# A hybrid decoder block on one core: two experts' weights loaded in shifted halves, the router's and the final norm's small loads moved, and the first tile's slots ahead of the second's

## The reference, cut to what matters

```python
h = concat(meta_tokens, x)                  # 16 + 256 positions of 1024
u = rmsnorm(h, norm_mix_w)
p = u @ w_in                                # 1024 x 7184: pool, q, k, v, z, a, b, two gates
merged = sigmoid(g_A) * pool_mixer(p) + sigmoid(g_B) * gated_deltanet(p)
h = h + merged @ w_out
u = rmsnorm(h, norm_ffn_w)
group  = argmax(softmax(u @ router_group_w + router_group_b))           # 4 groups
expert = top2(softmax((u @ router_expert_w + router_expert_b)[group]))  # 8 in the group
h = h + sum_e weight_e * ((silu(u @ w_gate[e]) * (u @ w_up[e])) @ w_down[e])   # 32 experts
out = rmsnorm(h, norm_final_w)[16:]         # all float32
```

## Time and profile before

| | us |
|---|---|
| median of three runs | 775.12 |
| the profiled execution's own time | 776.95 |
| span of the profile | 775.2 |
| TensorE busy | 748.8 (97%) |
| VectorE busy | 320.9 (41%) |
| ScalarE busy | 311.9 (40%) |
| GpSimd busy | 125.4 (16%) |
| DMA queue of SP, share of 16 engines | 81.2% |

### The profile page before, as it was taken

How to read it: one execution, slowest core, us unless ns; L and a number is a source line. 1 busy time by engine, 2 the same in 40 slices (tenths; PEclk the granted TensorE clock), 3 DMA queues, 4 the chain that set the end, 5 groups by cost and what they waited for, 6 DMA issues and landing times.

```text
span 775.2 us, 16094 instructions
## 1 busy us (share of the span) xinstructions
PE 748.8 (97%) x6512; PEld 536.1 (69%) x6512; DVE 320.9 (41%) x793; ACT 311.9 (40%) x632; POOL 125.4 (16%) x209
## 2 busy tenths in 40 slices
PE   8999999999999999899999999999999999998895
PEld 7989989998999988655555555565555555454452
DVE  4894687678675855822211311220221112111112
ACT  6975678586584744712212121222112121121123
POOL 7473242225433540000000000000000000000000
PEclk9999999999999999999999999999999999999999
DMA  8536556554754458999999999999999999999993
GB/s 204 147 87 165 152 135 160 138 151 110 181 147 125 140 193 309 414 400 424 420 427 428 428 427 428 425 429 426 428 427 427 428 427 426 429 426 426 424 416 137
DMA packets 83552, 241.06 MB, mean 311 GB/s; under 512 B 7185, under 2 KB 65666, under 8 KB 71826
## 3 DMA queue, kind: packets, MB, share of 16 engines
q1 hardware_dynamic: 83170, 239.19, 81.2%
q10 hardware_dynamic: 304, 0.79, 0.4%
HBM read 238.92 MB, written 1.05 MB: 310 GB/s over the span
## 4 chain that ended last, share of the span: by engine, by line
PE 80%; DMA 11%; issue 4%; DVE 4%; ACT 1%; POOL 0%; SPq 0%; DVEq 0%; POOLq 0%; ACTq 0%
PE banks L2158 23%; PE banks L1811 21%; PE banks L2216 12%; DMA ring<-in_expert_w_up_dram 10%; PE banks L2089 3%; PE banks L2171 3%; PE banks L2007 2%; PE banks L1931 1%; PE banks L2192 1%; PE banks L1944 1%; PE banks L1992 1%; PE banks L1935 1%; DMA x<-in_x_dram 1%; PE banks L1969 1%; PE banks L1948 1%
## 5 line engine op out<-in xcount | busy, mean ns | idle before, releaser
L2158 PE MATMUL banks<-ring,bench 128*64 128x256 f32 x2048 | 240.0, 388 | 8.4 <-DMA ring<-in_expert_w_up_dram 6.2
L2158 PEld LDWEIGHTS banks<-ring,bench 128*64 128x64 f32 x2048 | 146.6, 134 | 108.8 <-issue 21.0
L1811 PE MATMUL banks<-rounded 128*128 128x256 f32 (+2 forms) x1320 | 194.1, 294 | 0.0
L1811 PEld LDWEIGHTS banks<-rounded 128*128 128x128 f32 x1320 | 168.5, 189 | 3.1
L1714 DVE TENSOR_TENSOR bench<-banks,bench 128x256 f32<-128x256 f32 x32 | 13.6, 425 | 259.5 <-PE banks L2158 172.2
L2216 PE MATMUL banks<-ring,bench 128*64 128x512 f32 x512 | 116.9, 598 | 0.6 <-ACT bench L1096 0.5
L1107 ACT ACTIVATE ysb<-banks 64x512 f32<-64x512 f32 x63 | 37.2, 591 | 147.2 <-PE banks L2216 146.5
L2216 PEld LDWEIGHTS banks<-ring,bench 128*64 128x64 f32 x512 | 34.1, 136 | 63.2 <-issue 59.4
L875 ACT ACTIVATE rounded<-room 128x1024 fp32r<-128x1024 f32 x64 | 67.4, 1054 | 23.2 <-PE banks L1811 15.1
L1096 ACT ACTIVATE bench<-banks 128x256 f32<-128x256 f32 x32 | 12.3, 384 | 146.9 <-PE banks L2192 146.9
L1333 DVE TENSOR_TENSOR rounded<-room,rounded 128x1024 fp32r<-128x1024 f32 x49 | 61.6, 1259 | 16.5 <-ACT rounded L875 15.5
(11 more groups left out here) (312 smaller groups left out, 867.0 us busy)
## 6 DMA issues: line engine op xcount, KB each, us to landing
ring<-in_expert_w_down_dram SPq DMA_DIRECT2D x28, 2048.0 KB, 26.7
ring<-in_expert_w_gate_dram SPq DMA_DIRECT2D x27, 2048.0 KB, 25.6
ring<-in_expert_w_up_dram SPq DMA_DIRECT2D x27, 2048.0 KB, 26.8
room<-in_w_in_dram SPq DMA_DIRECT2D x56, 512.0 KB, 4.3
ring<-in_expert_w_up_dram SPq DMA_DIRECT2D x16, 512.0 KB, 7.1
ring<-in_expert_w_down_dram SPq DMA_DIRECT2D x16, 512.0 KB, 7.1
ring<-in_expert_w_gate_dram SPq DMA_DIRECT2D x12, 512.0 KB, 5.8
room<-in_w_out_dram SPq DMA_DIRECT2D x8, 512.0 KB, 4.5
```

The costliest lines, as they stand in the source:

```text
L1811: ins = T.matmul(o, a, b[:, k, lo_at:L], start=(k == 0 and n == 0), stop=(k == KT - 1 and n == 2))
L2158: ins = T.matmul(pb[5 + c][half * 64:half * 64 + SLOTS, 0:256], xgT[:, q % ROOMS, kt, j * SLOTS:(j + 1) * SLOTS], w[:, kt, half], start=(k ...
```

## The change: what it does

1. The final norm's gain is loaded as 8 columns (`gain_out`) at the start, and not spread by a DMA into `spare`. In experts 28 and 29 TensorE spreads it (`spread_gain`, 8 products each), and DVE copies it into `wfin`, which now lies in a part of `xgT` that is free by then.
2. The router's biases are loaded behind lands 10 and 11. The waits for biases and gains are one wait for four loads.
3. `FRONT_AFTER` lets the quarters of up 1 go one land earlier.
4. Chunks 9 to 14 (experts 3 and 4) are loaded in halves that are shifted by one half: 9a into `spare` after the logits, 9b into the first half of slot 0, 10a into its second half, and so on to 14b in the first half of slot 5. A semaphore `half` counts the first halves that TensorE has used.
5. In the router, DVE makes the first tile's slots before it picks for the second, the lows of tile 0 come before the slots of tile 1, and TensorE multiplies the first tile's high part before the second tile's place.

```diff
-ROUT = 5 * 16
+ROUT = 4 * 16
+SHIFTED = range(RING, RING + 6)          # RING = 9
+HALF_COUNTED = range(RING + 6)
-FRONT_AFTER = [61, 61, 62, 62]
+FRONT_AFTER = [60, 60, 61, 61]
+BIAS_AFTER = [10, 11]
...
+        def half_at(n, half, again):
+            if n in SHIFTED and not again:
+                at = 2 * (n - RING) + half - 1
+                if at < 0:
+                    return spare[:]
+            else:
+                at = 2 * (n % RING) + half
+            return ring[:, RING_AT[at // 2], at % 2 * CHUNK // 2:(at % 2 + 1) * CHUNK // 2]
...
+                if step == ("land", BIAS_AFTER[0]):
+                    sp.dma_start(rbias[:, 0:EXPERTS], router_expert_b[0:1, :].to_broadcast([P, EXPERTS])).then_inc(S("rout_land"), 16)
...
-                    sp.dma_start(rbias[:, 0:EXPERTS], router_expert_b[0:1, :].to_broadcast([P, EXPERTS])).then_inc(S("rout_land"), 16)
-                    sp.dma_start(rbias[:, EXPERTS:36], router_group_b[0:1, :].to_broadcast([P, GROUPS])).then_inc(S("rout_land"), 16)
-                    taken(sp, ("G", HEADS - 1))
-                    sp.dma_start(wfin, norm_final_w[None, :].to_broadcast([P, D])).then_inc(S("rout_land"), 16)
...
+                def used_up(n):
+                    sp.wait_ge(S(used[n % 3]), base + n // 3 + 1)
+                for n in range(3 * EXPERTS):
+                    e, c = n // 3, n % 3
+                    if n in SHIFTED and not again:
+                        if n == RING:
+                            sp.wait_ge(S("logits"), TT)
+                        else:
+                            used_up(n - RING - 1)
+                        if n >= RING + 3:
+                            sp.wait_ge(S(f"w_land{n - RING}"), 16 * loads_until(n - RING, False))
+                        load_half(sp, n, 0)
+                        sp.wait_ge(S("half"), n - RING + 1)
+                        load_half(sp, n, 1)
+                        continue
+                    if n >= RING:
+                        used_up(n - RING)
+                        if n - RING + 1 in SHIFTED and not again:
+                            sp.wait_ge(S("half"), n - RING + 2)
+                    elif again:
+                        sp.wait_ge(S(used[c]), base)
+                    if again or (e and (e, c) not in EARLY):
+                        load_chunk(sp, e, c)
...
             pick(0)
             inverse_rms(1)
+            first_slots(0)
             pick(1)
-            first_slots(0)
+            lows(0, front)
             first_slots(1)
-            for cols in (slice(0, 3 * D // PARTS), slice(3 * D // PARTS, D)):
-                for i in range(TT):
-                    lows(i, cols)
+            lows(1, front)
+            lows(0, rest)
+            lows(1, rest)
...
+                    elif j < GAIN_PARTS:          # DVE, experts 28 and 29
+                        dve.wait_ge(S("gathered"), parts + QUADS * PARTS + j + 1)
+                        V.tensor_copy(wfin[:, j * 512:(j + 1) * 512], pb[4][:]).then_inc(S("xgT"), 1)
...
             place(0)
             seed(0)
+            high_products(0)
             seed(1)
             place(1)
...
+                def spread_gain(n):
+                    pe.wait_ge(S("xgT"), parts + QUADS * PARTS + n - 2)
+                    for k in range(KT):
+                        ins = T.matmul(pb[4].rearrange("p (j k) -> p k j", k=KT)[:, k, :], gain_out[:, k:k + 1].to_broadcast([P, P]),
+                                       ident[:, n * 64:(n + 1) * 64], start=True, stop=True, skip_group_check=True)
+                    ins.then_inc(S("gathered"), 1)
...
                 def gather_first():
...
+                    pe.wait_ge(S("xlo"), 1)
+                    for part in range(PARTS - 1):
+                        first_products(xlo, part, 0)
+                    high_products(1)
+                    pe.wait_ge(S("xlo"), 2)
+                    for part in range(PARTS - 1):
+                        first_products(xlo, part, 1).then_inc(S("gathered"), 1)
...
                     for kt in range(KT):
...
-                        if first and (kt + 1) % (KT // QUARTERS) == 0 and kt < KT - 1:
-                            ins.then_inc(S("quarter"), 1)
+                        if kt == KT // 2 - 1 and 3 * e + c in HALF_COUNTED and not again:
+                            ins.then_inc(S("half"), 1)
...
                     turn_mid(e)
                     if q + 1 < QUADS:
                         gather(q + 1, j, 1)
+                    elif j < GAIN_PARTS:
+                        spread_gain(j)
```

More of the change, by code:

```diff
@@ L417, with loads_of, loads_until, loads_in_all @@
         LO_AT[_s[1]] = (_name, _i + 1)
-def uses(n, k, slots):
-    return (n - k + slots - 1) // slots
+def loads_of(n, again):
+    if (n // 3, n % 3) in PIECES or n < 3 and not again:
+        return 0
+    if n in SHIFTED and not again:
+        return 2
+    return QUARTERS if n in (3, 4) and not again else 1
+def loads_until(n, again):
+    return sum(loads_of(m, again) for m in range(n % RING, n + 1, RING))
+def loads_in_all(slot, again):
+    return sum(loads_of(m, again) for m in range(slot, 3 * EXPERTS, RING))
 def build_block(nc, x, meta_tokens, norm_mix_w, w_in, conv_w, pool_w, pool_scale, a_log, dt_bias, dn_norm_w,
@@ L812, in one_pass @@
                 again = not isinstance(ps, int)
[L813 to L821, removed]
-                                cols = slice(n * CHUNK // QUARTERS, (n + 1) * CHUNK // QUARTERS)
-                                slot = 3 * (e % RINGS) + c
-                                sp.dma_start(ring[:, RING_AT[slot], cols], (gate_v, up_v, down_v)[c][e][:, cols]).then_inc(S(f"w_land{slot}"), 16)
-                            continue
-                        if e >= RINGS:
-                            sp.wait_ge(S(used), base + (e - RINGS + 1))
-                        elif again:
-                            sp.wait_ge(S(used), base)
-                        if again or (e and (e, c) not in EARLY):
-                            load_chunk(sp, e, c)
@@ new lines, in one_pass @@
+                used = ("gate", "up", "y")
+                def used_up(n):
+                    sp.wait_ge(S(used[n % 3]), base + n // 3 + 1)
+                for n in range(3 * EXPERTS):
+                    e, c = n // 3, n % 3
+                    if n in SHIFTED and not again:
+                        if n == RING:
[16 more added lines that the diff above has]
+                        load_chunk(sp, e, c)
@@ L2130, in landed @@
-                    loads = ps * (uses(EXPERTS, e % RINGS, RINGS) - short) - (e % RINGS == 0)
-                    quarters = QUARTERS - 1 if e % RINGS == 0 or e % RINGS == 1 and (c < 2 or again or e > RINGS) else 0
-                    pe.wait_ge(S(f"w_land{3 * (e % RINGS) + c}"), 16 * (loads + quarters + (e // RINGS + 1)))
+                    n = 3 * e + c
+                    loads = loads_until(n, again)
+                    if again:
+                        first, other = (loads_in_all(n % RING, over) for over in (False, True))
+                        loads = ps * other + (first - other + loads)
@@ L2134, in gate_up @@
+                    pe.wait_ge(S(f"w_land{n % RING}"), 16 * loads)
                 def gate_up(e, c, name):
@@ L2210, in down @@
                         landed(e, 2)
[L2211 removed]
+                    ws = [half_at(3 * e + 2, n, again).rearrange("p (j d) -> p j d", j=2) for n in range(2)]
                     for j in range(4):
```

78 lines of the change are left out of this document (39 added, 39 removed).

## The result

| ten runs of each, same chip | median us | lowest to highest |
|---|---|---|
| kernel before | 775.27 | 774.88 to 776.66 |
| changed kernel | 777.63 | 776.65 to 779.07 |

The ratio is 1.003, with a 95% interval from 1.0022 to 1.0039: the change costs 2.3 us, between 1.7 and 3.0. The profiled execution of the changed kernel took 779.07 us (span 777.3), its slowest; the one of before took 776.95 (span 775.2). Both lie 1.4 to 1.8 above their medians, so the two traces can be set side by side; between them the span grew by 2.1 us. Chunk n is the load 3e + c of expert e, as in the code (c is 0 for gate, 1 for up, 2 for down); up 28 is the up matrix of expert 28, chunk 85. A landing is the start of an issue plus the view's time to landing, which has one decimal, so landings are good to 0.1 us.

A forecast was written before the change was run, and what follows sets the result against it. Expert-weight transfers were taken to bound the kernel, with TensorE's work after the last chunks behind them. Stream +0.2 and gain spreads +1.6 made +1.8 us on 775.12, giving 776.9 us, range 774.5 to 778.4.

The forecast's parts named there:

- the two terms of the sum: +0.2 us for the later stream of expert chunks and +1.6 us for TensorE's gain spreads at the end.
- Early loads: Router biases, gain and up 1 quarters issued earlier: covered by waits, 0 us, at most 0.4 for the biases.
- Router: New DVE order in the router: first gate product at 326.0 us, later by 0.1, between -0.3 and +0.4.
- Shifted halves up to chunk 17: Halves of chunks 9 to 14 end at 357.4 us; chunk 17, held, issued about 369.2, lands 376.6 against 376.5.
- The stream behind chunk 17: Chunks 18 to 22 come free in time, so +0.1 stays, plus 0.1 for a thin queue: +0.2 us.
- The final gain: TensorE's two spreads in experts 28 and 29, 1.76 us each; waits hide 1.9, +1.6 us reaches the end.
- I find no cheaper row: Pricing the gain spread: no profiled float32 product was cheaper than 0.103 to 0.134 us per record.
- A: Rival: half a chunk's lead survives because chunk 17 isn't held or TensorE arrives earlier; 775.4 us, chance 0.16.
- B: Rival: the gain spreads cost nothing, hidden by waits of experts 28 to 31; 775.3 us, chance 0.14.
- C: Rival: halves run slowly at 349 GB/s, 3.0 us each, chunk 17 lands at 378.0; 778.2 us, chance 0.10.
- A and B together: Rival: the stream gains 1.3 us and the spreads cost the tail nothing; 773.8 us, chance 0.08.
- The data wait behind 600 us: Sign: TensorE's first wait for expert weights after 600 us stays within 0.5 us of its old place.

The follow-up runs named there:

- both repairs: Changed kernel with the final gain spread by four transposes per half and chunks 18 to 22 loaded in halves, chunk 17 not held: 776.31 us against 775.40.

## Why the prediction came out near, point by point

The forecast was +1.8 us, 776.9; measured were +2.3 and +2.0, 777.6. Sign and range held, and so did the hold on chunk 17 and the spreads in the tail. But what the stream lost, it lost for the most part behind chunk 17, where the forecast had next to nothing, and the two terms of the sum were off in opposite directions. Part of the nearness is luck.

**Early loads, 0.** The issues came as foretold (quarters of up 1 at 286.30 and 291.68, the down pair at 311.86), and the kernel with them alone is within 0 to +1.4.

**Router, +0.1.** Foretold 326.0 for the first gate product, in the trace 325.82 with logits 0.16 earlier: +0.1. (The working had slips of a tenth: 1.02 us of lows from 321.6 end at 322.6, and 26 products of 0.14 us are 3.6 and not 3.5, which gives 326.2.) DVE did as worked out: slots of tile 0 at 318.74, lows at 321.38 and 322.90.

**Shifted halves up to chunk 17.** Half 9b was to land at 332.8 and did. The ten behind it were to end at 357.4 and ended at 359.3: 1.9 us were lost on the way. That changed little, because chunk 15 was to start at 359.4 by its issue. Then chunk 15 landed at 364.9 (foretold 364.3) and 16 at 370.3 (369.2); 17 was issued at 369.13 (369.2) and landed at 376.5 (376.6). The idle queue ahead of it shows in this window of the changed kernel:

```profile
368.00:370.00 2.00, 2.00 (x20) 1.24 (x18) 0.00 (x0) 0.49 (x1) 0.00 (x0) 1.00 0.20 82
```

**The stream behind chunk 17, +0.2: mis-sized.** The sentence that failed is "Chunks 18 to 22 come free at least 1 us before their turn, so this difference stays to the end", with its 0.1 for a thin queue. I asked only that the first byte come before the last byte of the chunk ahead. Behind whole chunks the traces want more. Over all fourteen traces, for whole chunks behind chunk 15, by how long before the landing of the chunk ahead they were issued (the loss is the distance of two landings less 4.9 us, from unrounded times):

| issued ahead by | chunks | lost, us |
|---|---|---|
| under 3.7 us | 14 | 1.1 to 2.5, each of them (all are chunk 17 or 19) |
| 3.7 to 4.2 | 5 | 0.0 to 0.2 (all are chunk 18, right behind a late 17) |
| 4.2 to 5.1 | 15 | 0.0 to 1.1; nine of them 0.3 or more |
| 5.1 to 6 | 8 | none |
| over 6 | 979 | mean 0.04; 50 of them 0.4 to 1.5 |

In the changed kernel chunk 19 was 3.3 ahead and lost 1.2, chunk 22 was 4.6 ahead and lost 1.0. In the kernel before, chunks 16 to 22 were issued 4.3 us or more ahead.

Chunk 15, which stands outside the table, shows that a lead is not the whole account. What lies ahead of it in the nine kernels with shifted halves is a half and not a whole chunk, and it was issued 2.6 to 3.4 us before that landed. In six of them it lost nothing, with leads of 3.0 to 3.4; in three it lost 0.7, 1.0 and 2.1, with 2.6, 2.7 and 3.0. And the second half of chunk 12, issued 5.4 to 5.9 us ahead, lost 0.4 to 1.6 in all nine. So a short lead can be enough, a longer one can fail, and no run varied the lead by itself: that a lead under 3.7 us costs a us is a regularity of chunks 17 and 19 here, not a limit of the queue. Why is open. That the queue's engines finish a chunk at different times would explain a part, but was only argued. The Trainium skill, "DMA: Bandwidth & Descriptors", section "Latency and other measured facts", tells of an HBM access latency of 0.2 us on average and 2 us at high load, and of a fixed cost of about 2 us; by that (an estimate) a lead of 3.1 us would have been enough. Chunk 15 in six traces agrees with that, chunk 17 without its hold does not (3.1 us ahead, 1.2 lost).

**How large the term is.** At up 28 the two traces of the changed kernel have 714.6 and 715.1, the two of the kernel before 713.3 and 713.5: +1.1 to +1.8, where I had +0.2 with +0.7 as the upper bound. But two of each are few. The variants that keep the halves and all holds, with the spreads left out or the router in its old order, have up 28 at 713.3 and 712.5. Over all traces the mean is 713.7 for the six with held chunks, 712.7 for the five with quarters, and 712.5 for the three with chunks 18 to 22 in halves. Counted from the issue of chunk 15, which takes out what was late before, it is 357.8, 356.8 and 357.2 us. The holds thus cost about 1.0 us in the mean, with a scatter in each group as large as that. The early loads brought the stream forward against issues that TensorE times, the holds moved the issues back, and the queue ran thin from both sides.

The medians bear the size less well still: with quarters, which have no holds, the median is no better than the changed kernel's. How much of the +2.0 to +2.3 the holds make is open.

**The final gain, +1.6: too high in the tail.** A spread took 1.71 us (1.76 foretold, 16 records of 0.107). Two are 3.4; the tail grew by 0.8 to 1.2 in every trace with them (62.7 to 63.0 us against 61.7 to 61.9). So 2.4 were hidden and not 1.9: in the trace the waits of up 29 and up 30 (0.77 and 0.36) and ACT's ahead of down 29 (0.26) are gone, as foretold, 1.4 together. The other 1.0 lay in stretches where the timeline lists no idle time, but products stood further apart before; I had put them at 0.5. So the gate and up products of expert 29, from the first start to the last end, took 8.40 us before, 0.77 of it the wait, and take 7.42 now. The term is +1.0 by the traces, below its bounds of 1.4 to 2.3. By the medians the gain alone costs +1.8 (+1.1 to +2.6), and leaving the spreads out wins nothing, so the two medians disagree with each other, and neither gives the 1.0 of the traces.

**The float32 records.** "I find no cheaper row" was right for a product of this form. But the operation has a cheaper form: four transposes are four records in 0.36 us, 0.09 each, where eight products are sixteen. The Trainium skill, "TensorE: Matmul & The Clock Gate", section "Part 4: PE-mode transpose", gives about 0.275 us for one of 128x128 (bf16) in a kernel's context; in a row of four they followed each other here after a third of that. The trace of before had such a row, and I overlooked it: the transposes of `turn_mid` are two records of 128 columns, and the next product starts 0.20 us behind the first.

```profile
717.77 0.44 PE L2192 MATMUL banks<-ident,bench 128*128 128x128 f32 x2 [0.58 <-DVE bench L1714]
717.97 0.48 PE L2171 MATMUL banks<-yhi,give 128*128 128x512 f32 x1
```

**Rivals.** A (the half's lead survives) fell: the hold is there, and without it the lead is lost all the same. B (spreads free) fell by the tail. C (halves slow by themselves) stood at 778.2, nearer to the measurement (0.6) than the forecast (0.7). Its mechanism came true in part: the halves took 2.65 us each, between the forecast's 2.46 and C's 3.0, at 395 GB/s, just above the 390 from which C decides. The slack ahead of chunk 15 took it all, and chunk 17 stayed bound by its issue. It was whole chunks, issued late, that lost. By the 341 GB/s of the page C's sum gives about 779.1, and not the 778.4 of the text. A and B together (773.8) fell with both.

**Signs.** The first gate product, the quarters, chunk 17 with the idle queue ahead of it, the two groups of 16 records and up 29 and up 30 without a wait came as listed. The data wait behind 600 us did not: I took it to be at 615 us, from the chain, where the timeline has 638.9, and it moved forward by 13.9 us to 625.0. That sign told of the late stream: all six traces with held chunks have this first wait at 623.8 to 625.6 us, and six of the eight others at 637.2 to 639.5 (the early loads alone and the first kernel with both repairs have 623.6 and 624.5). And the sixteenth slice of the earlier trace rows shows 8 tenths, not 9; nothing hangs on it.

**The sum.** By traces +1.1 to +1.8 and +0.8 to +1.2, together +1.9 to +3.0; by medians +2.0 to +2.3. What the experiments show is that both repairs together take most of it away (+0.4); that the two terms share it about evenly is read from traces, and no median shows either of them alone.

## What to carry to other kernels

For a queue that is to stay full, don't count on the time to the first byte alone: here 2 MB issued under 3.7 us before the end of a whole chunk lost over a us in 14 of 14 cases, though behind a half as short a lead did no harm in six of nine; over 5 us ahead whole chunks rarely lost. Loading earlier is worth nothing while the slots that follow are freed by the engine that computes: it turned a full queue into a thin one here. Look in the trace for a row of the operation, and not only of the instruction you have in mind, before you call a price the cheapest. And to spread a vector over the partitions, a transpose of its broadcast cost a fifth of the products by an identity here (0.36 us against 1.71).

## What the runs showed of the hardware besides

**A fall of TensorE's clock in two executions of fourteen.** The kernel before, the changed kernel run again, and the kernel with transposes alone, at 60 to 62 us (the clock is the third column from the end):

```profile
60.00:62.00 2.00, 2.00 (x11) 2.00 (x11) 0.00 (x0) 1.61 (x3) 1.78 (x3) 0.50 0.79 183
```

```profile
60.00:62.00 2.00, 2.00 (x11) 2.00 (x11) 0.00 (x0) 1.72 (x4) 1.75 (x4) 0.50 0.76 179
```

```profile
60.00:62.00 2.00, 2.00 (x20) 2.00 (x19) 0.00 (x0) 2.00 (x6) 1.83 (x3) 1.00 0.80 198
```

The granted clock was 0.50 (1.2 GHz) in the first two, behind an idle time of 0.7 us that all three have at 57 to 58 us. The same instructions took up to twice as long: counted from the first product behind that idle time, the two hundredth starts 17.5 us later, in the other twelve traces 15.9. Everything behind ran 1.6 us later for it: chunk 15 was issued at 356.8 and 357.0, where ten traces without it had 355.1 to 355.7 (the other two, at 356.7, had lost 1 us or so earlier on, at the full clock). In the kernel before it didn't reach the stream: chunk 17 landed at 376.5, in its two variants without the fall (early loads, new gain) at 376.7 and 376.0. The changed kernel's chunks 17, 19 and 22 wait for TensorE, so there such a delay is passed on: chunk 17 at 376.5 and 377.1 in its two late traces, 375.0 and 375.1 in two variants that hold it alike and weren't late (spreads left out, old router), though 377.7 in a third (transposes alone), where it lost 2.4 us.

**Pauses in a full stream.** The 50 chunks of 979 above come to about one in twenty. From chunk 23's landing to up 28's the fourteen traces took 306.0 to 307.9 us, a scatter nearly as large as the change's whole cost, and it limits what these comparisons can tell.
